# Low-rank products of the attention, with the weights stationary, one row group of x at a time

## The reference

```
m = silu(c) @ ada_w[0] + ada_b[0]          # c: one row of 1024; 6 outputs of 1024: shift, scale, gate, ...
hx = rmsnorm(x, norm_mix) * (1 + scale) + shift      # 512 x 1024, per token a norm, per column a scale
hc = the same for ctx, with c_ctx                    # 256 x 1024
q_lat, kv_lat, k_rope = split(hx @ mla_w_in, [384, 256, 64])
q = rmsnorm(q_lat) @ w_qb        # 8 heads of 192
kv = rmsnorm(kv_lat) @ w_kvb     # 8 heads of 128 + 128
the same kv_lat, k_rope and kv for hc (no queries)
```

## Time and profile before

| | us |
|---|---|
| median of 3 runs | 1593.66 |
| lowest, highest | 1592.88, 1593.67 |
| the profiled execution's own time | 1592.2 |
| its span | 1590.4 |

### The profile page before, as it was taken

The page is one execution under the profiler, slowest core; times in us unless marked ns, Lnnn a source line. Parts: engine busy times, 40 slices in busy tenths (PEclk is TensorE's granted clock), DMA queues, the critical chain, the costliest instruction groups (busy, mean ns, idle before and its releaser), DMA issues.

```text
span 1590.4 us, 15656 instructions
## 1 busy us (share of the span) xinstructions
PE 1454.8 (91%) x6490; PEld 678.2 (43%) x6490; DVE 668.4 (42%) x1161; ACT 232.3 (15%) x430; POOL 80.5 (5%) x72
## 2 busy tenths in 40 slices
PE   4999999999599999999989899999599999998987
PEld 2655656554233333332323588854133333333332
DVE  2576777433713232322322778734423232232223
ACT  3133453333300000000000300013100000000000
POOL 0010010000000000000000033000100000000000
PEclk9999999999889999999999999999699999999999
DMA  9933221496589999999999923452699999999996
GB/s 383 339 120 118 82 104 53 166 391 269 198 344 426 427 426 427 426 428 427 426 427 428 388 71 108 165 218 107 246 428 427 425 427 428 426 427 427 427 427 293
DMA packets 59248, 504.93 MB, mean 317 GB/s; under 512 B 7999, under 2 KB 8222, under 8 KB 29482
## 3 DMA queue, kind: packets, MB, share of 16 engines
q1 hardware_dynamic: 54928, 490.69, 75.1%
q0 software_dynamic: 2752, 8.92, 1.5%
q10 hardware_dynamic: 1498, 4.33, 0.7%
HBM read 497.62 MB, written 6.29 MB: 317 GB/s over the span
## 4 chain that ended last, share of the span: by engine, by line
PE 72%; DMA 20%; DVE 5%; ACT 2%; issue 1%; ACTq 0%; DVEq 0%; POOLq 0%
PE ps L1011 31%; DMA work<-in_exp_w_up_dram 11%; PE ps L1095 9%; PE ps L870 7%; DMA ring<-in_exp_w_up_dram 6%; PE ps L1027 5%; PE ps L617 3%; PE ps L777 3%; PE ps L736 3%; PE ps L679 2%; PE ps L675 2%; PE ps L740 1%; PE ps L763 1%; DMA work<-in_ada_w_dram 1%; PE ps L1049 1%; PE ps L995 1%
## 5 line engine op out<-in xcount | busy, mean ns | idle before, releaser
L1011 PE MATMUL ps<-ring,work 128*64 128x512 f32 x1824 | 409.2, 598 | 31.2 <-ACT work L1355 13.0
L1011 PE MATMUL ps<-work 128*64 128x512 f32 x1248 | 282.5, 601 | 20.9 <-ACT work L1355 8.9
L1890 DVE TENSOR_TENSOR work<-ps,work 128x1024 f32<-128x1024 f32 x120 | 141.3, 1219 | 283.1 <-PE ps L1027 283.1
L1011 PEld LDWEIGHTS ps<-ring,work 128*64 128x64 f32 x1824 | 127.5, 137 | 294.2 <-issue 250.4
L1011 PEld LDWEIGHTS ps<-work 128*64 128x64 f32 x1248 | 87.4, 138 | 202.2 <-issue 172.1
L1027 PE MATMUL ps<-work 64*128 64x512 f32 x480 | 119.3, 615 | 0.0
L1908 DVE SCALAR_TENSOR_TENSOR work<-ps,gate_e,gate_ffn 128x512 f32<-128x512 f32 x32 | 24.0, 751 | 185.8 <-PE ps L1011 185.8
L1901 DVE TENSOR_TENSOR work<-work,ps 128x512 f32<-128x512 f32 x32 | 22.0, 687 | 176.1 <-issue 151.8
L1351 ACT ACTIVATE work<-ps 128x512 f32<-128x512 f32 x32 | 19.1, 597 | 487.3 <-PE ps L1011 487.3
L2078 POOL DMA_INDIRECT work<-xn_rows,row_no x32 | 30.6, 956 | 1036.5 <-PE ps L995 733.2
L1355 ACT ACTIVATE work<-ps 128x512 f32<-128x512 f32 x32 | 19.1, 597 | 372.8 <-PE ps L1049 372.8
(11 more groups left out here) (306 smaller groups left out, 1355.3 us busy)
## 6 DMA issues: line engine op xcount, KB each, us to landing
ring<-in_exp_w_gate_dram SPq DMA_DIRECT2D x38, 2048.0 KB, 31.7
ring<-in_exp_w_up_dram SPq DMA_DIRECT2D x37, 2048.0 KB, 32.4
ring<-in_exp_w_down_dram SPq DMA_DIRECT2D x37, 2048.0 KB, 33.6
work<-in_exp_w_up_dram SPq DMA_DIRECT2D x27, 2048.0 KB, 31.5
work<-in_exp_w_gate_dram SPq DMA_DIRECT2D x24, 2048.0 KB, 34.8
work<-in_exp_w_down_dram SPq DMA_DIRECT2D x23, 2048.0 KB, 36.8
ring<-in_ada_w_dram SPq DMA_DIRECT2D x32, 1024.0 KB, 7.0
ring<-in_ada_w_dram SPq DMA_DIRECT2D x6, 2048.0 KB, 7.6
```

The costliest lines, as they stand in the source:

```text
L1011: last = mm(PS[64 * h:64 * h + 64, bank, :], lhsT[:, m * P + 64 * j:m * P + 64 * j + 64], slot_rows[sl][:, m, h * BANK:(h + 1) * BANK], st ...
L1890: v.tensor_tensor(row, PS[:, b:b + 2, :], row, ALU.add).then_inc(added[L], 1)
```

## The change

The low-rank products of x are turned round: the weights of one row group (5 blocks of 128 columns: 3 of queries, 2 of keys and values) are stationary and the 512 columns of the x tokens are moving, into five PSUM banks that stay open over all 8 row groups. The results come with the rank as rows, so the latents are not transposed any more.

The conditioning weights are loaded by row group (FIRST_TILES: groups of 1, 1, 2, 2, 2 row groups), each with all 1024 rows and only its own 128 or 256 columns of shift and of scale. first_product_of(u) makes the shift and scale of those row groups, first_T(u) turns them, first_take(u) applies them to the turned x, which now lies unmodulated in hT, and low_rank(m, parts) follows for row group m. The loads of mla_w_in are cut in three (WIN_CUTS). x is loaded first, in two halves; the context comes after the last conditioning load, and the small vectors are issued by SP.

The rotary columns (64) have products of their own, low_rank_kr, with the token tiles stationary. The norms of the latents come from ScalarE's squares of the five banks, summed over the rank by products with a column of ones (the loops before ssq_done); the reciprocal roots are no longer applied to the latents but to the projections, in the take of pair 0. VectorE's slices stand among the context steps. The loads of w_qb and w_kvb come after the last slice; the rotary tables and biases behind them.

The core of the diff (blank lines left out; of removed functions, the listing above has the text):

```diff
-    FIRST_LOADS = 4
+    FIRST_TILES = [(0, 1), (1, 1), (2, 2), (4, 2), (6, 2)]
+    FIRST_LOADS = len(FIRST_TILES)
...
-        lat = view(W, 18432, 2, LAT)
+        lat_sq = [view(W, 14336 + n * T, T) for n in range(QC + KVC + 1)]
...
-        first_ada = [view((R[0], W)[u // 2], (u % 2) * 2 * GROUP, 2, GROUP) for u in range(FIRST_LOADS)]
+        first_ada = [view(t, lo, 2 * KC, nk * P) for (t, lo), (_, nk) in zip(
+            ((R[0], 0), (R[0], GROUP), (R[0], 2 * GROUP), (W, 0), (W, 2 * GROUP)), FIRST_TILES)]
...
+            def load_first(u):
+                k0, nk = FIRST_TILES[u]
+                for kind in range(2):
+                    lo = kind * D + k0 * P
+                    sp.dma_start(first_ada[u][:, kind * KC:(kind + 1) * KC, :], ada_w[0, :, lo:lo + nk * P].rearrange("(k p) n -> p k n", p=P)
+                                 ).then_inc(ada_in[(u + 3) % 4], 16)
+            def load_w_in(n):
+                lo, hi = WIN_CUTS[n], WIN_CUTS[n + 1]
+                sp.dma_start(w_in[:, lo:hi, :], mla_w_in[0, lo * P:hi * P, :].rearrange("(k p) n -> p k n", p=P)).then_inc(win_in[n], 16)
+            load_first(0)
+            load_w_in(0)
+            load_first(1)
+            load_first(2)
+            load_w_in(1)
+            load_first(3)
+            load_w_in(2)
+            sp.wait_ge(ada_main, 1)
+            load_first(4)
             sp.dma_start(rows_in[:, 0:CT, :], ctx[0].rearrange("(t p) d -> p t d", p=P)).then_inc(rows_in_s[0], 16)
...
+            def load_slice(k):
+                sp.dma_start(ada_slice[k % 3], ada_w[0, k * P:(k + 1) * P, 2 * D:4 * D]).then_inc(ada_in[k % 3], 16)
+            sp.wait_ge(ada_main, 3)
+            load_slice(0)
+            load_slice(1)
+            sp.wait_ge(ada_main, 4)
+            load_slice(2)
+            for k in range(3, KC):
+                sp.wait_ge(slice_added, k - 2)
+                load_slice(k)
+            sp.wait_ge(ada_main, FIRST_LOADS)
+            sp.dma_start(w_qb, mla_w_qb[0].rearrange("(k p) n -> p k n", p=P)).then_inc(wq_in, 16)
+            sp.dma_start(w_kvb, mla_w_kvb[0].rearrange("(k p) n -> p k n", p=P)).then_inc(wkv_in, 16)
...
+            def first_product_of(u):
+                k0, nk = FIRST_TILES[u]
+                pe.wait_ge(ada_in[(u + 3) % 4], 32 * (u // 4 + 1))
+                for m in range(KC):
+                    for g in range(2 * nk):
+                        last = mm(PS[32 * g:32 * g + 32, 6, 0:P], cond_T[:, m, :],
+                                  first_ada[u][:, g // nk * KC + m, (g % nk) * P:(g % nk + 1) * P], start=m == 0, stop=m == KC - 1)
+                last.then_inc(ada_main, 1)
+            def first_T(u):
+                rows = 64 * FIRST_TILES[u][1]
+                pe.wait_ge(ada_rows, u + 1)
+                if u == 0:
+                    pe.wait_ge(setup_out, 2)
+                else:
+                    pe.wait_ge(ada_out, u)
+                tr(PS[:, 7, 3 * P:3 * P + rows], ada_part[0][0:rows, (u % 4) * P:(u % 4 + 1) * P], ident[0:rows, 0:rows]
+                   ).then_inc(ada_sum, 1)
...
+            def x_T(t):
+                pe.wait_ge(xn_in, t + 1)
+                for h in range(2):
+                    if t == XT - 1:
+                        pe.wait_ge((inT_a, inT_d)[h], 1)
+                    for q in range(4):
+                        last = tr(PS[:, (2 * t + h) % 6, q * P:(q + 1) * P], rows_in[:, CT + t, (4 * h + q) * P:(4 * h + q + 1) * P], ident)
+                    last.then_inc(inT, 1)
...
+            def low_rank(m, parts):
+                if m in WIN_CUTS:
+                    pe.wait_ge(win_in[WIN_CUTS.index(m)], 16)
+                pe.wait_ge(inT_d, MODULATED + m + 1)
+                for c in parts:
+                    last = mm(PS[:, c, :], w_in[:, m, c * P:(c + 1) * P], hT[:, m, CX:KEYS], start=m == 0, stop=m == KC - 1)
+                    if m == KC - 1:
+                        last.then_inc(lat_done, 1)
+            def low_rank_kr(tiles):
+                for n, j in enumerate(tiles):
+                    for m in range(KC):
+                        last = mm(PS[:, 5, n * ROPE:(n + 1) * ROPE], hT[:, m, j * P:(j + 1) * P], w_in[:, m, QL + KVL:LAT],
+                                  start=m == 0, stop=m == KC - 1)
+                last.then_inc(lat_done, 1)
+            Q_PARTS, KV_PARTS = range(QC), range(QC, QC + KVC)
...
+            first_product_of(0)
+            x_T(XT - 1)
+            first_T(0)
+            for u, (k0, nk) in enumerate(FIRST_TILES):
+                ahead = u + 1 < FIRST_LOADS
+                if nk == 2:
+                    low_rank(k0, range(QC + KVC))
+                if not ahead:
+                    context_T(0)
+                    context_T(1)
+                low_rank(k0 + nk - 1, [0])
+                if ahead:
+                    first_product_of(u + 1)
+                low_rank(k0 + nk - 1, [1, 2])
+                if ahead:
+                    first_T(u + 1)
+                else:
+                    context_T(2)
+                    context_T(3)
+                low_rank(k0 + nk - 1, KV_PARTS)
+            low_rank_kr(range(CT, NT))
+            pe.wait_ge(inT_d, MODULATED + KC + 4)
+            for c in range(KVC):
+                for m in range(KC):
+                    last = mm(PS[:, 6, c * CX:(c + 1) * CX], w_in[:, m, QL + c * P:QL + (c + 1) * P], hT[:, m, 0:CX],
+                              start=m == 0, stop=m == KC - 1)
+            last.then_inc(lat_done, 1)
+            pe.wait_ge(lat_a, KV_SQ)
+            pe.wait_ge(lat_d, X_TAKEN)
+            for t in range(XT):
+                for c in Q_PARTS:
+                    mm(PS[:, 1, t:t + 1], lat_sq[c][:, t * P:(t + 1) * P], ones, start=c == 0, stop=c == QC - 1)
+                for c in KV_PARTS:
+                    last = mm(PS[:, 1, XT + t:XT + t + 1], lat_sq[c][:, t * P:(t + 1) * P], ones, start=c == QC, stop=c == QC + KVC - 1)
+            last.then_inc(ssq_done, 1)
+            pe.wait_ge(lat_a, KR_TAKEN)
+            low_rank_kr(range(CT))
+            pe.wait_ge(lat_a, CTX_SQ)
+            for t in range(CT):
+                for c in range(KVC):
+                    last = mm(PS[:, 0, t:t + 1], lat_sq[QC + KVC][:, c * CX + t * P:c * CX + (t + 1) * P], ones,
+                              start=c == 0, stop=c == KVC - 1)
+            last.then_inc(ssq_done, 1)
+            pe.wait_ge(lat_d, CTX_TAKEN)
+            pe.wait_ge(wq_in, 16)
...
+            for t in range(XT):
+                j = CT + t
+                if t % 2 == 0:
+                    act.wait_ge(rows_in_s[1 + t // 2], 16)
+                own.link(f(junk_in, rows_in[:, j, :], ACT.Square, accum_out=stat[:, j:j + 1]))
+                f(stat[:, 8 + j:9 + j], stat[:, j:j + 1], ACT.Sqrt, bias=eps, scale=1.0 / D).then_inc(std_in, 1)
+            def raw_T(t):
+                act.wait_ge(inT, 2 * t + 1)
+                f(hT[:, 0:4, CX + t * P:CX + (t + 1) * P], PS[:, 2 * t % 6, :].rearrange("p (a b) -> p a b", a=4),
+                  ACT.Copy).then_inc(inT_a, 1)
+            def first_rows(u):
+                rows = 64 * FIRST_TILES[u][1]
+                act.wait_ge(ada_main, u + 1)
+                f(ada_part[0][0:rows, (u % 4) * P:(u % 4 + 1) * P], PS[0:rows, 6, 0:P], ACT.Copy).then_inc(ada_rows, 1)
...
+            raw_T(XT - 1)
+            for u in range(1, FIRST_LOADS):
+                first_rows(u)
...
-                f(dst, PS[:, 6, 0:dst.shape[1]], ACT.Copy).then_inc(proj_a, 1)
+                f(dst, PS[:, 6, 0:dst.shape[1]], ACT.Copy, scale=stat[:, r_of(s):r_of(s) + 1]).then_inc(proj_a, 1)
...
+            def raw_T(t):
+                dve.wait_ge(inT, 2 * t + 2)
+                v.tensor_copy(hT[:, 4:8, CX + t * P:CX + (t + 1) * P], PS[:, (2 * t + 1) % 6, :].rearrange("p (a b) -> p a b", a=4)
+                              ).then_inc(inT_d, 1)
+            normalize_rows(CT, 1)
+            normalize_rows(CT + 1, 2)
+            raw_T(0)
+            normalize_rows(CT + 2, 3)
+            raw_T(1)
+            normalize_rows(CT + 3, 4)
+            raw_T(2)
...
+            raw_T(XT - 1)
...
+            def first_take(u):
+                k0, nk = FIRST_TILES[u]
+                ks = slice(k0, k0 + nk)
+                dve.wait_ge(ada_sum, u + 1)
+                bias = vec[:, V_ADA:V_ADA + 2 * KC].rearrange("p (n k) -> p n k", n=2)[:, :, ks].unsqueeze(3).to_broadcast([P, 2, nk, 2])
+                v.tensor_tensor(modv[0][0][:, :, ks, :],
+                                PS[:, 7, 3 * P:3 * P + 64 * nk].rearrange("p (n k r) -> p n k r", n=2, k=nk)[:, :, :, 0:2],
+                                bias, ALU.add).then_inc(ada_out, 1)
+                dve.wait_ge(ada_out, u + 1)
+                v.scalar_tensor_tensor(out=scl[0][0][:, ks, :], in0=modv[0][0][:, 1, ks, :], scalar=1.0,
+                                       in1=col(V_NM + k0, nk, 2), op0=ALU.add, op1=ALU.mult).then_inc(mod_ready, 1)
+                dve.wait_ge(mod_ready, u + 1)
```

(34 more changed lines are left out.)

317 lines of the change are left out of this document (108 added, 209 removed).

## The result

| | before | changed |
|---|---|---|
| median us | 1593.66 | 1603.6 |
| lowest, highest | 1592.88, 1593.89 | 1601.89, 1604.38 (4 runs) |
| profiled execution | 1592.2 | 1604.26 |
| its span | 1590.4 | 1602.4 |

The change makes the kernel slower: ratio of the times 1.0062, 95% interval [1.0044, 1.0079]. A later comparison of the unchanged pair gave 1603.46 and 1.0070 [1.0057, 1.0083]. Forecast were 1600.0 and a range of 1589 to 1607; the median lies inside it, 3.6 above the forecast.

The account below looks back on a forecast made before the run. Front bound by TensorE, expert stages by a weight stream. Start 25.0 plus dense part 71.6 puts the first projection at 96.6 against 90.13, net +6.3: 1592.2 + 6.3 = 1598.5, plus 1.5 to the median, 1600.0; range 1589 to 1607.

Parts of the forecast that it names:

- The start: First low-rank product on TensorE: begins at 25.0 us, 13.3 earlier than before; 23 to 27 by clock.
- The dense part: TensorE from first low-rank product to first projection: terms sum to 71.6 us, putting the first projection at 96.6.
- The disputed price: Rotary and sum products on TensorE: stationary loads not hidden, 0.115 us a record, near 0.23 a product.
- The first rival: Stationary loads hide behind TensorE's products, so small products cost only their columns: net -4.2 us, 1589.5; chance 0.20.
- The Trainium skill's figure: Some 25 ns for a product of 1 to 64 columns: the 24 sums 1.2 us instead of 5.5, time 1595.7.
- The clock: TensorE half clock after the 2 us gap before the new start: costs 1.6 us (0 to 3).
- The prediction's second reckoning: Net +6.3 us restated: 13.3 of earlier start against conditioning, rotary, sums, waits, transposes and clock, less latent transposes.
- The later wait: TensorE's VectorE wait at 118.7 to 121.3 and its clock drop disappear, giving 3.4 us back: 1596.6; chance 0.18.
- The small pieces: Conditioning loads in small pieces starve the low-rank products below 216 GB/s; at 190, 5 us late, 1605; chance 0.07.
- The estimate of 252 GB/s: DMA rate for first loads in 512-byte pieces, at 0.0325 us a packet; 1 KB pieces 315 GB/s.
- the slope: DMA packet time carried on from 0.0198 us at 182 bytes and 0.0274 at 379 bytes.
- What comes behind: Stages after the first projection stay as long as now, so the shift of the front comes through whole.

Follow-up runs that it names:

- the kernel with four sums: Changed kernel with one sum-of-squares product per x tile instead of five (4 instead of 20), part of the computation left out: 1593.39 us, ratio 1.0008.
- all conditioning first: Changed kernel with all five conditioning products and their transposes ahead of the first low-rank product: 1618.23 us, ratio 1.0158.
- both kinds shortened: Changed kernel with squares added on VectorE before the sums and rotary columns stationary, in pairs: 1592.27 us, ratio 0.9998.
- The repetition of the changed kernel: The changed kernel itself, unmodified, timed again against the kernel before: 1603.46 us, ratio 1.0070.
- the filled gap: Changed kernel with two discarded 512-column products in the 1.7 us wait before the first low-rank product: 1603.11 us, ratio 1.0068.
- dense products between: Changed kernel with a discarded 512-column product before each x tile's sums: 1609.1 us, ratio 1.0099.
- the short context rotary: Changed kernel with the context's rotary products cut to the first row group (2 in place of 16), sums whole: 1599.54 us, ratio 1.0036.
- added squares: Changed kernel with squares added on VectorE first, 8 one-column products in place of 20 and 2 of 4: 1598.07 us, ratio 1.0033.
- stationary rotary columns: Changed kernel with the 64 rotary columns stationary, tokens moving, even and odd row groups in two array halves: 1598.43 us, ratio 1.0030.
- 1595 or 1607: Changed kernel with each x tile's sums moved among the second half of the context low-rank products: median 1601.46 us, ratio 1.0065, six times.

## Why the prediction was right, and where it was not

The forecast outcome (slower by more than 0.2%, given 0.60) came, and the mechanism held in the main: an earlier start, paid for with conditioning products that were free, rotary products cut loose and sums of squares. That the number was near is in part luck, since a clock term five times too small stood beside a start that was forecast too late. By its own steps:

- *The start.* 25.0 was forecast, 23.00 measured. The three turned tiles, with their waits for VectorE inside, end at 17.4, not 18.1. The other 1.3 come mostly from the vectors' small transposes, the first conditioning product (1.94) and the last tile (1.09): they run at full speed, where partly half had been taken. The wait for VectorE, 1.7 us, was there as reckoned.
- *The dense part.* 71.6 was forecast, 75.98 measured (98.98 - 23.00). From starts of the timeline, group by group, forecast in brackets: x low-rank 35.7 (34.4), conditioning products 1 to 4 8.9 (7.8), small transposes 0.5 (0.6), context transposes 2.0 (2.1) with a wait of 1.05 (1.6), x rotary 7.1 (7.4), context low-rank 7.0 (6.9), sums 7.0 (5.5), context rotary 6.9 (3.7), and inside them what had a term of its own, the clock (1.6).
- *The small products.* The disputed price was right. At the full clock 64 rotary records take 7.1 us, 0.111 each (0.115 forecast), and a tile of five sums takes 1.11 us, 0.111 a record again: 64 columns and one column cost the same with a new stationary operand of 128 columns each, while a one-column record with 32 stationary columns took 0.02: it is the stationary load that is paid. The first rival, hidden loads (1589.5), is out. The Trainium skill's figure cited with it ("TensorE: Matmul & The Clock Gate", Back-to-back issue gap; 25 ns) is one for isolated products, which by that section leaves the stationary load out; it does not describe these f32 products. The prediction also applied it to the sums alone: on the 96 rotary records as well, the same estimate would have come to about 1587 (11.1 - 2.4 less than 1595.7).
- *The clock: the step that failed.* "The gap of 2 us just before the new start is of that kind; I take 1.6 (0 to 3)." This term was mis-sized, beyond its own bounds. Around the start the profiled execution lost 1.7, half of the 3.4 us from 23.7 to 27.1, as forecast, though that stretch comes and goes. What was missing is the second stretch, where TensorE has no gap at all. Of the 6.96 and 6.87 for sums and context rotary, 5.34 (24 x 0.223) and 3.6 (from 84.44 to 88.05 in the kernel with four sums) are what they take at the full clock: 4.9 lost before the first projection, and 1.6 in the projections. So 8.2 us stand against 1.6. Without the clock the dense part took 69.4 (75.98 - 1.7 - 4.9), where the other terms had come to 70.0. The step looked at gaps alone, since the trace of before has half clock only near gaps.
- *Why 1600.0 was still near.* To the forecast of +6.3 the first projection added 2.4 (+5.0 of clock, -2.0 start, -0.6 other terms) and the projections 1.6: +10.3, with medians 9.9 apart. With the 1.5 us that the prediction adds from the profiled execution of before to its median, 1592.2 + 10.3 + 1.5 = 1604.0, and 1603.6 was measured. (The prediction's second reckoning, "put otherwise", adds up to 6.0 and not to 6.3; nothing hangs on it.)
- *The later wait* (second rival). It is unchanged, and the half clock behind it too (132.9 to 139.8, 3.4 us lost): the forecast's view, that nothing is given back there, is right.

```profile
131.64 1.09 PE L797 MATMUL ps<-ident,ring 128*128 128x128 f32 x8 [2.59 <-DVE work L1741]
```

- *The small pieces* (third rival). Loads 2 to 4 were forecast for 26, 35 and 45; with all conditioning first, where TensorE stands before them, they release it at 24.8, 32.7 and 42.3. In the changed kernel TensorE waits for no DMA between 23 and 125 us. The waits of that stretch, all of them (total, times, longest):

```profile
PE ps L655 <- DVE ring L1535: 1.7, 1, 1.7
PE ps L646 <- DVE ring L1570: 1.0, 1, 1.0
PE ps L797 <- ACT work L1315: 0.6, 1, 0.6
```

The estimate of 252 GB/s for 512 bytes was too low: from 14 to 17 us, with packets of 533 bytes on average, the engines moved 302 GB/s, and from 12 to 20 us, with 792 bytes, 330. The time of one packet was about as reckoned (0.043 us at 792 bytes, 112.3% of 8 us x 16 over 3332; the slope gives 0.043), but the packets' times add up to more than the engines' whole time, and that the estimate did not have:

```profile
q1 hardware_dynamic: 3332, 2.64, 112.3%
```

- *What comes behind.* Stages behind 360 us are as long as before within 0.2 us up to the end of the first expert stage. That the shift comes through whole was also shown by conditioning first: between the profiled executions the first projection moved by 12.6 and the time by 14.0 (1618.23 against 1604.26); 0.8 of the rest is in the projections (10.42 against 9.58).

What the experiments settle: that most of the mis-sized term goes with the narrow products (4 of 20 sums left: 10 us gone for 3.6 of work; both kinds shortened: 11 us gone for 5.3, of which 3.0 in the sums and 3.7 in the rotary products, less 1.4 of waits); that wide products put among them don't hold the clock in every execution; that shortening one kind by half gains about 4 to 5 us and leaves the clock falling in some or all executions.

Not every run of narrow products brings the clock down. The x rotary products, 64 records of 64 columns in 7.1 us at the same 0.111 each, stand in eight profiles besides that of the changed kernel, and none of the nine has a fall in them or before the sums. The repetition of the changed kernel (69.60 to 76.69):

```profile
70.00:80.00 10.00, 10.00 (x78) 9.61 (x78) 10.00 (x12) 1.82 (x5) 0.00 (x0) 1.00 0.98 357
```

The late fall comes only once the one-column sums have begun: 2.4 to 5.6 us after, in the changed kernel, its repetition, and the kernels with the filled gap, dense products between, conditioning first, the short context rotary, added squares and stationary rotary columns. What stays open is whether the one-column products are special, or what stands around them counts as well; why the same program holds the clock in one execution and not in the next (1595 or 1607); and what amount of narrow work is still safe.

## What to carry to other kernels

A reordering that fills TensorE is to be priced product by product with the stationary load as the floor: here 0.111 us a record, whether 64 columns follow or one. A sequence of such narrow products, the one-column ones above all, can also cost the clock, without any gap; here this cost 6.5 us (4.9 and 1.6), more than the 5.3 of the sums themselves. Put narrow columns on the stationary side, add partial sums on another engine, and look at the granted clock before and behind them. One profile and a median can mislead where the times of one program spread: look at all of them. When an order is tightened, ask what was behind the moved load in its queue: twice a wait taken from TensorE came back through a DMA that VectorE stood for.

## What the runs showed that I had not expected

- The granted clock fell from 2.4 to 1.2 GHz while TensorE was 100% busy, and stayed low for 13.6 us (88.6 to 102.2) and 17 us (86.1 to 103.1) in two executions of the same program. It came back during the projections behind.
- The times of one program can fall in two groups, 1595.28 to 1596.48 and 1606.45 to 1607.76, with mean clocks of 0.981 and 0.973 to 0.975.
- Loads mostly in 512-byte and 1 KB pieces moved at 318 GB/s (15 to 20 us) to 364 (20 to 25 us), where 426 was reached later (102 to 104 us, projection stage).
